# Seven edits at the stage boundaries of a fused two-block transformer kernel: first transfers, row sums, squares, and the order of the first slab

## The chip, the core and the metric

One NeuronCore of a Trainium2 chip runs the whole program. Its engines are TensorE (PE, with its weight loads as PEld), VectorE (DVE), ScalarE (ACT), GpSimd (POOL) and SyncE (SP); each runs its own instructions in order, and they wait for one another on semaphores. Weights come from HBM by DMA, which SP's and POOL's queues issue. The metric is the device time of one launch in microseconds (us), as the median of some runs; lower is better. Traces come from one further execution under the hardware profiler.

## The reference: what is computed

A token matrix of 256 x 1024 goes through two blocks of two layers each. Every sublayer has the form "norm over the 1024 features, matmul up, something in the middle, matmul down, add to x". All is float32.

```python
D_MODEL = 1024; SEQ = 256; DEPTH = 2; D_FF = 2816

def rms_norm(x, g):
    x32 = x.astype(jnp.float32)
    y = x32 * lax.rsqrt(jnp.mean(x32 * x32, axis=-1, keepdims=True) + EPS)
    return (y * g.astype(jnp.float32)).astype(x.dtype)

# first block, layer l: mixer (pool + attention, or RG-LRU), then the conv FFN
x = x + mixer(rms_norm(x, norm_mix[l]), ...)
z = causal_dwconv(rms_norm(x, norm_ffn[l]) @ w_in, conv_w, conv_b); u, g = jnp.split(z, 2, axis=-1)
x = x + (jax.nn.gelu(g) * u) @ w_out

# second block, layer i
cond = jax.nn.silu(c)
mod = (cond @ w_mod[i] + b_mod[i]).reshape(-1, N_SUBLAYERS, 3, D_MODEL)     # 1024 -> 9216
h = rms_norm_2(x, g) * (1.0 + scale[:, None, :]) + shift[:, None, :]        # modulate
x = x + 0.5 * gate * ((jax.nn.silu(h @ w_gate) * (h @ w_up)) @ w_down)      # FFN, before and after
x = x + gate * ssd_mixer(h)          # layer 0; mla_mixer(h) in layer 1
```

## The kernel before

**Layout.** x is kept transposed in SBUF as `X`, 128 partitions x 8 feature tiles x 256 tokens. The weights of all 22 matmul stages are cut into 271 slabs of 1 MB (128 x 2048). A slab has four times a place in the ring `raw` (4 buffers, filled by SP), then a high part `hi` made by ACT (`split_hi`, L814, two halves) and a low part `lo = raw - hi` made by DVE (`split_lo`, L1259, two halves), both in rings of 2. Each product is three matmuls: high weight x high input, high x low, low x high (`three`, L312 to L314); the four gated stages take high and low input side by side in one 512-wide matmul (`wide`, L347, L349). A slab is 48 such 256-wide products, or 16 wide and 16 narrow ones.

**Stages in order.** pa_in (8 slabs), pa_out (4), f0_up (22), f0_down (11), rg_in (10), rg_out (5), f1_up (22), f1_down (11), g00_up (22), g00_down (11), ssd_in (25), ssd_out (8), g01_up (22), g01_down (11), g10_up (22), g10_down (11), mla_in (3), mla_uq (4), mla_ukv (2), mla_out (4), g11_up (22), g11_down (11).

**A norm** stands ahead of ten of them (pa_in, f0_up, rg_in, f1_up, g00_up, ssd_in, g01_up, g10_up, mla_in, g11_up). ACT squares the eight tiles of X into `S` as the residual adds deliver them (L840, three pairs and two single tiles). DVE adds tiles 2,3 and then 4,5 to tiles 0,1 (`fold_squares`, L1278); in the code this stands ahead of the residual adds of the last two tiles (k = 3). PE sums over the features with one-column matmuls of tiles 0, 1, 6, 7 (L457; the trace has two records for each, 16 in all). ACT takes the root (L845), DVE the reciprocal and a diagonal matrix R, PE spreads it (L461). Then tile by tile DVE scales (L1346), ACT makes the high part (`xh_ready`, L851 or L853) and DVE the low part (`x_ready`, L1337 or L1339), and PE's first slab of the stage (`first_up_slab`, `gated_stage`) waits tile by tile for `x_ready`. pa_out and mla_out have no norm; there ACT and DVE make the two parts of the concatenated heads in pairs of tiles (L962 with `cat_hi`, L1501).

**A down stage** accumulates in PSUM banks 4 to 7; in its last slab PE finishes the outputs in pairs, and DVE adds each pair to X (`residual`, L1307, L1311, L1315). **The row sums** are `cond @ w_mod`: 144 units of 128 x 1024, each one a DVE instruction over a row of `modw` and `cond` (L1363), whose 512 KB come by SP through a ring of 3. They have no engine of their own and are spread over other stages by `MODS_PER`; `units_after` tells SP behind which slab the loads stand. In a down stage DVE does two after the split of every slab, the last of them after slab number SLABS-1, right ahead of the residual.

**The start.** SP issues X, the constants `CN`, the parameters `PAR`, four slabs and three row-sum units; POOL issues `cond`, positions and three tables. ACT, DVE and PE first wait until X, CN and PAR have all landed (`par_loaded`, 48).

## Time and profile before

| | us |
|---|---|
| median of 3 runs | 1985.22 (1983.73 to 1986.84) |
| the profiled execution, its whole time | 1992.79 |
| its span, first to last instruction | 1991.0 |
| PE busy | 1848.0 (93%) |
| DVE busy | 1440.8 (72%) |
| ACT busy | 1012.1 (51%) |
| TensorE clock granted, mean over the span | 0.943 of full |

PE is busy almost throughout; what is left is in short waits. The chain of waits, followed back from the last instruction, lies on PE for 85% of the span, on DVE for 8% and on ACT for 3%. A row of the timeline gives start, duration, engine, line, operation and, in brackets, how long the engine had been idle and what ended that. The granted clock is 1.00 (2.4 GHz) or 0.50 (1.2 GHz).

### The profile page before, as it was taken

The page shows a single profiled execution, that of the slowest core. Times are in us where ns is not written, and L with a number is a line of the kernel's source. Part 1 is how long each engine was busy: PE and PEld are TensorE (multiplying, and loading weights), DVE is VectorE, ACT ScalarE, POOL GpSimd, SP SyncE. Part 2 cuts the span into 40 slices and gives each one's busy share as a digit, 9 for nine tenths or more (in the row PEclk, how much of TensorE's full clock was granted, in tenths as well). Part 3 has the DMA queues.
Part 4 walks back from the last instruction along what each step waited for, and adds up shares of the span by engine and source line. Part 5 has one row for each costly group of instructions (what it writes and reads, how often), then busy time and mean ns, then how long its engine had stood idle before and what let it go on. Part 6 is the DMA issues. An engine that isn't in the chain of part 4 may idle for free.

```text
span 1991.0 us, 31981 instructions
## 1 busy us (share of the span) xinstructions
PE 1848.0 (93%) x12790; PEld 1697.5 (85%) x12790; DVE 1440.8 (72%) x2317; ACT 1012.1 (51%) x1582; POOL 18.5 (1%) x22
## 2 busy tenths in 40 slices
PE   6789999957999999999998999999999988899999
PEld 6579999857999888989996698889788987578899
DVE  4747888667788788889966758888888553656664
ACT  4445554563554455445557735553555344355542
POOL 2000000000000000000000000000000000000000
PEclk9799999888999999999998999999899977699999
DMA  8314459422455867884441035779577532014552
GB/s 311 116 43 167 172 193 348 156 106 85 170 187 213 317 228 263 307 321 170 174 166 42 1 127 190 268 287 364 200 276 287 209 107 105 22 43 169 184 180 101
DMA packets 61436, 367.15 MB, mean 184 GB/s; under 512 B 6832, under 2 KB 6832, under 8 KB 26384
## 3 DMA queue, kind: packets, MB, share of 16 engines
q1 hardware_dynamic: 60768, 362.67, 49.9%
q0 software_dynamic: 560, 3.01, 0.4%
q8 instruction: 71, 1.16, 0.2%
q14 instruction: 37, 0.30, 0.0%
HBM read 364.61 MB, written 1.05 MB: 184 GB/s over the span
## 4 chain that ended last, share of the span: by engine, by line
PE 85%; DVE 8%; ACT 3%; DMA 2%; issue 1%; SPq 0%; DVEq 0%; ACTq 0%
PE psum L347 17%; PE psum L312 16%; PE psum L313 16%; PE psum L314 16%; PE psum L349 9%; DVE lo L1259 2%; PE psum L660 1%; PE psum L470 1%; PE psum L611 1%; PE psum L494 1%; PE psum L711 1%; PE psum L457 1%; DMA modw<-wmod_dram 1%; ACT hi L814 1%; PE psum L482 1%
## 5 line engine op out<-in xcount | busy, mean ns | idle before, releaser
L1259 DVE TENSOR_TENSOR lo<-raw,hi 128x1024 fp32r<-128x1024 f32 x542 | 642.1, 1225 | 257.2 <-ACT hi L814 257.1
L814 ACT ACTIVATE hi<-raw 128x1024 fp32r<-128x1024 f32 x542 | 543.1, 1051 | 480.6 <-PE psum L314 475.8
L347 PE MATMUL psum<-XHL,hi 128*128 128x512 f32 x1408 | 505.9, 404 | 7.4 <-DVE XHL L1339 7.4
L312 PE MATMUL psum<-XHL,hi 128*128 128x256 f32 x1648 | 480.0, 291 | 20.5 <-DVE XHL L1337 7.1
L313 PE MATMUL psum<-XHL,hi 128*128 128x256 f32 x1648 | 474.2, 288 | 0.0
L314 PE MATMUL psum<-XHL,lo 128*128 128x256 f32 x1648 | 473.8, 287 | 0.0
L349 PE MATMUL psum<-XHL,lo 128*128 128x256 f32 x1408 | 399.0, 283 | 0.0
L312 PE MATMUL psum<-HH,hi 128*128 (+1 forms) x1264 | 361.4, 286 | 5.3 <-DVE lo L1259 5.3
L313 PE MATMUL psum<-HL,hi 128*128 (+1 forms) x1264 | 359.7, 285 | 0.0
L314 PE MATMUL psum<-HH,lo 128*128 (+1 forms) x1264 | 359.6, 284 | 0.0
L312 PEld LDWEIGHTS psum<-XHL,hi 128*128 128x128 f32 x1648 | 324.8, 197 | 26.7 <-issue 22.3
L347 PEld LDWEIGHTS psum<-XHL,hi 128*128 128x128 f32 x1408 | 268.7, 191 | 77.2 <-issue 9.8
L313 PEld LDWEIGHTS psum<-XHL,hi 128*128 128x128 f32 x1648 | 324.9, 197 | 1.3 <-issue 1.0
L314 PEld LDWEIGHTS psum<-XHL,lo 128*128 128x128 f32 x1648 | 324.4, 197 | 0.0
L349 PEld LDWEIGHTS psum<-XHL,lo 128*128 128x128 f32 x1408 | 270.1, 192 | 0.0
L312 PEld LDWEIGHTS psum<-HH,hi 128*128 128x128 f32 x1264 | 245.0, 194 | 5.9 <-issue 5.5
L313 PEld LDWEIGHTS psum<-HL,hi 128*128 128x128 f32 x1264 | 244.9, 194 | 0.1
L314 PEld LDWEIGHTS psum<-HH,lo 128*128 128x128 f32 x1264 | 244.7, 194 | 0.0
L1363 DVE CUSTOM_DVE_ANT_0 modw<-modw,cond 128x1024 f32<-128x1024 f32 x144 | 174.5, 1220 | 22.1 <-DMA modw<-wmod_dram 22.0
L907 ACT ACTIVATE S<-psum 128x512 f32<-128x512 f32 x88 | 52.6, 598 | 232.0 <-PE psum L349 232.0
L1434 DVE TENSOR_TENSOR S<-psum,S 128x512 f32<-128x512 f32 x88 | 60.9, 692 | 82.3 <-ACT S L907 82.0
L1403 DVE SCALAR_TENSOR_TENSOR S<-psum,PAR,S 128x254 f32<-128x254 f32 (+1 forms) x176 | 72.5, 474 | 0.0
(271 smaller groups left out, 1552.2 us busy)
## 6 DMA issues: line engine op xcount, KB each, us to landing
raw<-slabs_dram SPq DMA_DIRECT2D x271, 1024.0 KB, 4.8
modw<-wmod_dram SPq DMA_DIRECT2D x144, 512.0 KB, 5.8
A<-small_dram POOLq DMA_DIRECT2D x1, 1536.0 KB, 13.4
X<-x_dram SPq DMA_DIRECT2D x1, 1024.0 KB, 4.8
out_dram<-X SPq DMA_DIRECT2D x4, 256.0 KB, 2.3
cond<-cvec_dram POOLq DMA_DIRECT2D x1, 512.0 KB, 7.6
A<-tab_dram POOLq DMA_DIRECT2D x1, 512.0 KB, 16.7
PAR<-par_dram SPq DMA_DIRECT2D x1, 448.0 KB, 8.7
```

Of the source, the lines that this page charges most:

```text
L312: mm(dst, wh, xh, start=start, stop=False, skip_group_check=True)
L313: mm(dst, wh, xl, start=False, stop=False, skip_group_check=True)
L314: return mm(dst, wl, xh, start=False, stop=False, skip_group_check=True)
L347: mm(dst, hi[:, k, j * P:(j + 1) * P], XHL[:, kt, :, :].rearrange("p a t -> p (a t)"), start=start, stop=False, skip_group_check=True)
L349: return mm(dst[:, T:2 * T], lo[:, k, j * P:(j + 1) * P], XHL[:, kt, 0, :], start=False, stop=False, skip_group_check=True)
L457: last = mm(sums[:, j:j + 1], S[:, m * T + j * P:m * T + (j + 1) * P], ones[:, 0:1], start=(m == 0 and j == 0), stop=False, skip_group_che ...
L814: f(hi[:, n % SPLIT, at], raw[:, n % RAW, at], ACT.Copy).then_inc(q["hi_ready"], 1)
L907: f(S[:, 1024 + s % 2 * 512:1536 + s % 2 * 512].rearrange("p (a t) -> p a t", a=2), psum[:, b:b + 2, T:2 * T], ACT.Copy).then_inc(q["half_ ...
L1259: v.tensor_tensor(lo[:, n % SPLIT, at], raw[:, n % RAW, at], hi[:, n % SPLIT, at].bitcast(F32), ALU.subtract).then_inc(q["lo_ready"], 1)
L1363: v.tensor_tensor_reduce(out=w, in0=w, in1=cond[:, :], scale=1.0, scalar=0.0, op0=ALU.mult, op1=ALU.add, accum_out=MOD[:, n:n + 1]).then_i ...
L1403: last = stt(out=z, in0=bank[n % 4][:, m * T:(m + 1) * T - tap], scalar=col(f"fconv{layer}", (2 - tap) * 44 + k, i, 4), in1=z, op0=ALU.mul ...
L1434: v.tensor_tensor(two(dst), psum[:, b:b + 2, 0:T], two(S[:, 1024 + s % 2 * 512:1536 + s % 2 * 512]), ALU.add).then_inc(evacuated[s % 2], 1)
```

## The change

- **First transfers.** X comes in four parts of two tiles with a semaphore each, then the identity and ones columns of CN, slab 0 in two halves, PAR, slab 1, the rest of CN, slabs 2 and 3 and the row-sum units. POOL issues its five transfers after slab 1 has landed. ACT squares each pair as it lands; the copies to `identr`, `selr`, `maskr` (DVE) and the silu of `cond` (ACT) go behind slab 1 of pa_in.
- **Row sums.** A down stage does none behind its last split; ssd_out takes two after each of its first five splits, so that the 144 units still fit.
- **Squares.** DVE folds tiles 2,3 alone; PE sums tiles 0, 1, 4, 5, 6, 7: 12 one-column matmuls for 8.
- **First slab of a stage.** For tile kt PE takes the two products with the high input as soon as `xh_ready` (or `cat_hi`) allows, and the product with the low input of tile kt-1 behind it. In the gated stages the 512-wide matmul of the first slab becomes two of 256.

```diff
         "g10_up": "g10_down", "g11_up": "g11_down"}
-MODS_PER = {"f0_down": 2, "f1_down": 2, "g00_up": 2, "g00_down": 2, "g01_up": 2, "g01_down": 2,
+MODS_PER = {"f0_down": 2, "f1_down": 2, "g00_up": 2, "g00_down": 2, "ssd_out": 2, "g01_up": 2, "g01_down": 2,
             "g10_up": 2, "g10_down": 2}
...
         slabs, first = SLABS[name], N0[name]
-        last = [first + s + 2 for s in range(slabs - 2)] if name.endswith("down") else \
+        last = [first + s + 2 for s in range(slabs - 3)] if name.endswith(("down", "out")) else \
                [min(first + 2 * p + 3, NSLABS - 1) for p in range(slabs // 2)]
...
         @block.sync
         def _(sp):
-            sp.dma_start(X[:], x).then_inc(q["par_loaded"], 16)
-            sp.dma_start(CN[:], con).then_inc(q["par_loaded"], 16)
+            for k in range(4):
+                sp.dma_start(X[:, 2 * k:2 * k + 2, :], x[:, 2 * k:2 * k + 2, :]).then_inc(x_loaded[k], 16)
+            sp.dma_start(CN[:, 0:2 * P], con[:, 0:2 * P]).then_inc(q["ident_loaded"], 16)
+            sp.dma_start(raw[:, 0, 0:HALF], slabs[0][:, 0:HALF]).then_inc(q["slab_begun"], 16)
+            sp.dma_start(raw[:, 0, HALF:], slabs[0][:, HALF:]).then_inc(raw_loaded[0], 16)
             sp.dma_start(PAR[:], par).then_inc(q["par_loaded"], 16)
+            sp.dma_start(raw[:, 1, :], slabs[1]).then_inc(raw_loaded[1], 16)
+            sp.dma_start(CN[:, 2 * P:], con[:, 2 * P:]).then_inc(q["con_loaded"], 16)
             def load(k, n, i=None):
...
                 last.then_inc(q["slab_used"], 1)
+            def high_ready(preps, kt):
+
+                if preps in (2, 12):
+                    pe.wait_ge(q["cat_hi"], 4 * (preps // 12) + kt // 2 + 1)
+                else:
+                    pe.wait_ge(q["xh_ready"], KD * (norms[0] - 1) + kt + 1)
+
             def first_up_slab(stage, preps):
                 n = N0[stage]
                 pe.wait_ge(q["lo_ready"], 2 * n + 2)
-                for kt in range(KD):
-
-                    pe.wait_ge(q["x_ready"], KD * (preps - 1) + kt + 1)
-                    for m in range(2):
-                        last = three(bank[n % 4][:, m * T:(m + 1) * T], n, m * KD + kt,
-                                     XH[:, kt, :], XL[:, kt, :], start=(m == 0 and kt == 0))
+                b, k = bank[n % 4], n % SPLIT
+                for kt in range(KD + 1):
+                    if kt < KD:
+
+                        high_ready(preps, kt)
+                        for m in range(2):
+                            at = slice((m * KD + kt) * P, (m * KD + kt + 1) * P)
+                            for w in (hi, lo):
+                                mm(b[:, m * T:(m + 1) * T], w[:, k, at], XH[:, kt, :],
+                                   start=(m == 0 and kt == 0 and w is hi), stop=False, skip_group_check=True)
+                    if kt:
+
+                        pe.wait_ge(q["x_ready"], KD * (preps - 1) + kt)
+                        for m in range(2):
+                            at = slice((m * KD + kt - 1) * P, (m * KD + kt) * P)
+                            last = mm(b[:, m * T:(m + 1) * T], hi[:, k, at], XL[:, kt - 1, :],
+                                      start=False, stop=False, skip_group_check=True)
                 last.then_inc(q["slab_used"], 1)
             def wide(n, s, m, kt, start):
...
                 pe.wait_ge(q["lo_ready"], 2 * n + 2)
-                for kt in range(KD):
-                    pe.wait_ge(q["x_ready"], KD * (preps - 1) + kt + 1)
-                    for m in range(2):
-                        last = wide(n, 0, m, kt, kt == 0)
+                for kt in range(KD + 1):
+                    if kt < KD:
+
+                        high_ready(preps, kt)
+                        for m in range(2):
+                            at = slice((m * KD + kt) * P, (m * KD + kt + 1) * P)
+                            for w, half in ((hi, 0), (lo, T)):
+                                mm(psum[:, m, half:half + T], w[:, n % SPLIT, at], XH[:, kt, :],
+                                   start=(kt == 0 and half == 0), stop=False, skip_group_check=True)
+                    if kt:
+
+                        pe.wait_ge(q["x_ready"], KD * (preps - 1) + kt)
+                        for m in range(2):
+                            at = slice((m * KD + kt - 1) * P, (m * KD + kt) * P)
+                            last = mm(psum[:, m, T:2 * T], hi[:, n % SPLIT, at], XL[:, kt - 1, :],
+                                      start=False, stop=False, skip_group_check=True)
                 last.then_inc(q["slab_used"], 1)
                 for s in range(1, 4):
                     gated_slab(stage, s)
...
-                for m in (0, 1, 6, 7):
-                    if m >= 6:
+                for m in (0, 1, 4, 5, 6, 7):
+                    if m >= 4:
                         pe.wait_ge(q["squares_ready"], 8 * k + m + 1)
...
-            pe.wait_ge(q["par_loaded"], 48)
+            pe.wait_ge(q["ident_loaded"], 16)
             pe.wait_ge(q["zero_ready"], 1)
             norm()
...
                 if n >= NSLABS:
                     return
-                act.wait_ge(raw_loaded[n % RAW], plus(16 * (n // RAW + 1), i, 16))
+                if n == 0:
+                    act.wait_ge(q["slab_begun"], 16)
+                else:
+                    act.wait_ge(raw_loaded[n % RAW], plus(16 * (n // RAW + 1), i, 16))
                 if n >= SPLIT:
                     act.wait_ge(q["slab_used"], plus(n - SPLIT + 1, i, 4))
                 for h in range(2):
                     at = slice(h * HALF, (h + 1) * HALF)
+                    if n == 0 and h:
+                        act.wait_ge(raw_loaded[0], 16)
                     f(hi[:, n % SPLIT, at], raw[:, n % RAW, at], ACT.Copy).then_inc(q["hi_ready"], 1)
...
                         act.wait_ge(q["resid_ready"], 8 * (k - 1) + m + w)
+                    elif m < 7:
+                        act.wait_ge(x_loaded[m // 2], 16)
                     f(S[:, m * T:(m + w) * T], X[:, m:m + w, :].rearrange("p a t -> p (a t)"),
...
             act.wait_ge(q["zero_ready"], 1)
-            act.wait_ge(q["par_loaded"], 48)
-            norm("pa_in", then=ACT.Silu)
-            act.wait_ge(q["cond_loaded"], 16)
-            f(cond[:, :], cond[:, :], ACT.Silu).then_inc(q["cond_ready"], 1)
...
                     f(VRAW[:, 2 * (s - 6):2 * (s - 5), :],
                       bank[s % 4][:, :].rearrange("p (a t) -> p a t", a=2), ACT.Copy).then_inc(evacuated[s % 2], 1)
+                if s == 1:
+                    act.wait_ge(q["cond_loaded"], 16)
+                    f(cond[:, :], cond[:, :], ACT.Silu).then_inc(q["cond_ready"], 1)
                 if 3 <= s <= 6:
...
                     if s in between:
                         between[s]()
-                    modulation(mods)
+                    if s < SLABS[stage] - 3:
+                        modulation(mods)
             def fold_squares(k):
-                for pair in (1, 2):
-                    dve.wait_ge(q["squares_ready"], 8 * k + 2 * pair + 2)
-                    last = v.tensor_tensor(S[:, 0:2 * T], S[:, 0:2 * T], S[:, 2 * pair * T:2 * (pair + 1) * T],
-                                           ALU.add)
-                    if pair == 1:
-                        step.link(last)
-                last.then_inc(q["squares_folded"], 1)
+                dve.wait_ge(q["squares_ready"], 8 * k + 4)
+                v.tensor_tensor(S[:, 0:2 * T], S[:, 0:2 * T], S[:, 2 * T:4 * T],
+                                ALU.add).then_inc(q["squares_folded"], 1)
...
-            dve.wait_ge(q["par_loaded"], 48)
-            v.tensor_copy(identr[:, :], ident)
-            v.tensor_copy(selr[:, :], con_mat("select", 64))
-            v.tensor_copy(maskr[:, :], CN[:, CON["mask_f"]:CON["mask_f"] + 2 * P]).then_inc(q["identr_ready"], 1)
             fold_squares(0)
             split_lo(0)
+            dve.wait_ge(q["ident_loaded"], 16)
+            dve.wait_ge(q["par_loaded"], 16)
             norm("pa_in", "nmix0")
...
             for s in range(8):
                 split_lo(s + 2)
+                if s == 1:
+                    dve.wait_ge(q["con_loaded"], 16)
+                    v.tensor_copy(identr[:, :], ident)
+                    v.tensor_copy(selr[:, :], con_mat("select", 64))
+                    v.tensor_copy(maskr[:, :], CN[:, CON["mask_f"]:CON["mask_f"] + 2 * P]).then_inc(q["identr_ready"], 1)
                 if 3 <= s <= 6:
                     dve.wait_ge(q["qk_sum"], s - 2)
...
             group_rest(SSD_G - 1)
-            down_stage("ssd_out")
+            down_stage("ssd_out", mods=MODS_PER["ssd_out"])
             residual("ssd_out", 8)
...
             step.link(g.memset(UP[:, :, :, 0:PAD], 0.0))
+            pool.wait_ge(raw_loaded[1], 16)
             pool.dma_start(cond[:, :], cvec).then_inc(q["cond_loaded"], 16)
             pool.dma_start(posi[:, :], pos).then_inc(q["late_loaded"], 16)
```

What the change moves on three engines:

SP's queue at the program's start; X, CN, PAR, raw (the slabs) and modw (row-sum units) are the SBUF targets. Before:

```order
1 L274 DMA X<-x_dram 128x2048
2 L275 DMA CN<-con_dram 128x835
3 L276 DMA PAR<-par_dram 128x896
4 L285 DMA raw<-slabs_dram 128x2048 x4
5 L287 DMA modw<-wmod_dram 128x1024 x3
6 L282 DMA raw<-slabs_dram 128x2048 [waits lo_ready] x37
```

and now:

```order
1 L276 DMA X<-x_dram 128x512 x4
2 L277 DMA CN<-con_dram 128x256
3 L278 DMA raw<-slabs_dram 128x1024
4 L279 DMA raw<-slabs_dram 128x1024
5 L280 DMA PAR<-par_dram 128x896
6 L281 DMA raw<-slabs_dram 128x2048
7 L282 DMA CN<-con_dram 128x579
8 L291 DMA raw<-slabs_dram 128x2048 x2
9 L293 DMA modw<-wmod_dram 128x1024 x3
10 L288 DMA raw<-slabs_dram 128x2048 [waits lo_ready] x37
```

X stands in four parts, slabs 0 and 1 are ahead of or between PAR and the larger part of CN, and the transfers of row-sum units stay behind slab 3.

PE at the start of pa_in, from the last of the one-column matmuls over S, over the spread of R, into the first slab (psum<-XHL,hi and psum<-XHL,lo are high and low weights). Before:

```order
5 L457 MATMUL psum<-CN,S 128x1 [waits squares_ready]
6 L457 MATMUL psum<-CN,S 128x1
7 L461 MATMUL psum<-R,CN 128x256 [waits diag_ready]
8 L312 MATMUL psum<-XHL,hi 128x256 [waits x_ready,lo_ready]
9 L313 MATMUL psum<-XHL,hi 128x256
10 L314 MATMUL psum<-XHL,lo 128x256
11 L312 MATMUL psum<-XHL,hi 128x256
12 L313 MATMUL psum<-XHL,hi 128x256
13 L314 MATMUL psum<-XHL,lo 128x256
14 L312 MATMUL psum<-XHL,hi 128x256 [waits x_ready]
```

and now:

```order
9 L492 MATMUL psum<-CN,S 128x1 [waits squares_ready]
10 L492 MATMUL psum<-CN,S 128x1
11 L496 MATMUL psum<-R,CN 128x256 [waits diag_ready]
12 L357 MATMUL psum<-XHL,hi 128x256 [waits xh_ready,lo_ready]
13 L357 MATMUL psum<-XHL,lo 128x256
14 L357 MATMUL psum<-XHL,hi 128x256
15 L357 MATMUL psum<-XHL,lo 128x256
16 L357 MATMUL psum<-XHL,hi 128x256 [waits xh_ready]
17 L357 MATMUL psum<-XHL,lo 128x256
18 L357 MATMUL psum<-XHL,hi 128x256
19 L357 MATMUL psum<-XHL,lo 128x256
20 L364 MATMUL psum<-XHL,hi 128x256 [waits x_ready]
```

The first matmul of the slab waits for `xh_ready` in place of `x_ready`, and the first wait for `x_ready` comes after eight matmuls. The same order stands at every first slab. Where one listing of the norm had 8 rows of one-column matmuls it now has 12.

DVE at the end of f0_down, from the last row-sum units into the residual (X<-psum,X), the fold (S<-S) and the norm of rg_in. Before:

```order
265 L1259 TENSOR_TENSOR lo<-raw,hi 128x1024 x2
266 L1363 ISA modw,MOD<-modw,cond 128x1024
267 L1363 ISA MOD 128x1
268 L1363 ISA modw,MOD<-modw,cond 128x1024
269 L1363 ISA MOD 128x1
270 L1259 TENSOR_TENSOR lo<-raw,hi 128x1024
271 L1307 TENSOR_TENSOR X<-psum,X 128x512 x3
272 L1278 TENSOR_TENSOR S<-S 128x512 x2
273 L1311 TENSOR_TENSOR X<-psum,X 128x256 x2
274 L1259 TENSOR_TENSOR lo<-raw,hi 128x1024
```

and now:

```order
261 L1303 TENSOR_TENSOR lo<-raw,hi 128x1024 x2
262 L1404 ISA modw,MOD<-modw,cond 128x1024
263 L1404 ISA MOD 128x1
264 L1404 ISA modw,MOD<-modw,cond 128x1024
265 L1404 ISA MOD 128x1
266 L1303 TENSOR_TENSOR lo<-raw,hi 128x1024 x3
267 L1348 TENSOR_TENSOR X<-psum,X 128x512 x3
268 L1322 TENSOR_TENSOR S<-S 128x512
269 L1352 TENSOR_TENSOR X<-psum,X 128x256 x2
270 L1303 TENSOR_TENSOR lo<-raw,hi 128x1024
```

The two row-sum units behind the last full split are gone, and one of the two folds.

## Rows read from the trace of the kernel before

**Rows 1.** the page: the chain that ended last, by engine, share of the span

```profile
PE 85%; DVE 8%; ACT 3%; DMA 2%; issue 1%; SPq 0%; DVEq 0%; ACTq 0%
```

**Rows 2.** timeline from the start to pa_in's first matmul: start, us, engine, line

```profile
10.39 1.28 ACT L835 ACT_TABLE_LOAD   x1 [10.39 <-DMA PAR<-par_dram]
...
14.53 3.54 PE L457 MATMUL psum<-CN,S 128*128 128x1 f32 x16 [14.53 <-DVE S L1278]
...
15.92 2.00 ACT L814 ACTIVATE hi<-raw 128x1024 fp32r<-128x1024 f32 x2 [1.86 <-DMA raw<-slabs_dram]
...
18.11 0.26 ACT L845 ACTIVATE tiny<-psum,tiny 128x2 f32<-128x2 f32 x1 [0.18 <-PE psum L457]
...
19.74 2.00 ACT L814 ACTIVATE hi<-raw 128x1024 fp32r<-128x1024 f32 x2 [1.37 <-DMA raw<-slabs_dram]
...
20.02 1.22 PE L461 MATMUL psum<-R,CN 128*128 128x256 f32 x2 [1.95 <-DVE R L1329]
...
23.02 0.55 PE L312 MATMUL psum<-XHL,hi 128*128 128x256 f32 x1 [1.78 <-DVE XHL L1337]
```

**Rows 3.** transfers: KB each and us to landing; windows (us, PE busy, clock, DMA share, GB/s)

```profile
X<-x_dram SPq DMA_DIRECT2D x1, 1024.0 KB, 4.8
out_dram<-X SPq DMA_DIRECT2D x4, 256.0 KB, 2.3
...
10.00:14.00 4.00, 0.00 (x0) 1.00 1.02 431
...
26.00:30.00 4.00, 4.00 (x36) 1.00 1.03 420
```

**Rows 4.** timeline at the end of rg_out and the start of f1_up

```profile
489.66 0.75 DVE L1311 TENSOR_TENSOR X<-psum,X 128x256 f32<-128x256 f32 x2
...
489.80 1.95 PE L457 MATMUL psum<-CN,S 128*128 128x1 f32 x16 [0.94 <-DVE S L1278]
492.81 0.70 PE L461 MATMUL psum<-R,CN 128*128 128x256 f32 x2 [1.07 <-DVE R L1329]
...
494.07 1.20 ACT L851 ACTIVATE XHL<-S 128x256 fp32r<-128x256 f32 x3
...
495.30 0.55 PE L312 MATMUL psum<-XHL,hi 128*128 128x256 f32 x1 [1.78 <-DVE XHL L1337]
```

**Rows 5.** timeline at the end of f0_down and the start of rg_in

```profile
344.05 1.23 DVE L1363 CUSTOM_DVE_ANT_0 modw<-modw,cond 128x1024 f32<-128x1024 f32 x1 [2.24 <-DMA modw<-wmod_dram]
...
348.38 1.42 DVE L1278 TENSOR_TENSOR S<-S 128x512 f32<-128x512 f32 x2 [0.16 <-ACT S L840]
...
349.86 3.32 PE L457 MATMUL psum<-CN,S 128*128 128x1 f32 x16 [2.17 <-DVE S L1278]
...
357.25 0.55 PE L312 MATMUL psum<-XHL,hi 128*128 128x256 f32 x1 [1.78 <-DVE XHL L1337]
```

**Rows 6.** the one-column sums after f1_down, g00_down and pa_out

```profile
690.48 2.67 PE L457 MATMUL psum<-CN,S 128*128 128x1 f32 x16 [2.28 <-DVE S L1278]
...
889.58 1.95 PE L457 MATMUL psum<-CN,S 128*128 128x1 f32 x16 [1.82 <-DVE S L1278]
...
149.45 1.95 PE L457 MATMUL psum<-CN,S 128*128 128x1 f32 x16 [0.42 <-DVE S L1278]
```

**Rows 7.** windows around f0_down's end and f1_up's start (PE, PEld, DVE, ACT, POOL; clock; DMA)

```profile
347.70:350.15 2.45, 0.29 (x3) 0.30 (x3) 2.26 (x5) 1.25 (x3) 0.00 (x0) 1.00 0.66 269
350.16:353.20 3.04, 3.02 (x15) 2.93 (x14) 1.44 (x2) 0.75 (x2) 0.00 (x0) 0.50 0.12 16
...
495.30:500.30 5.00, 5.00 (x23) 5.00 (x24) 5.00 (x13) 3.46 (x7) 0.00 (x0) 0.50 0.10 36
```

**Rows 8.** timeline at pa_out's first slab

```profile
122.72 2.19 ACT L962 ACTIVATE XHL<-CAT 128x512 fp32r<-128x512 f32 x4
...
124.29 0.35 PE L312 MATMUL psum<-XHL,hi 128*128 128x256 f32 x1 [3.21 <-DVE XHL L1501]
```

**Rows 9.** timeline of DVE in ssd_out, one slab's split

```profile
1170.68 2.36 DVE L1259 TENSOR_TENSOR lo<-raw,hi 128x1024 fp32r<-128x1024 f32 x2 [3.40 <-ACT hi L814]
```

10 lines of the change are left out of this document (7 added, 3 removed).

## The prediction

> **What bounds the kernel now.** I read the page first, then the timeline of the places that the diff names, then the granted clock in windows. The chain by engine [rows 1] lies on PE for 85%: inside a stage PE is the bound, and nothing off PE is worth anything there. So I look only at where PE has nothing to do, and every edit aims at such a place. At the start, PE's first product of pa_in comes at 23.02 us, behind a string of waits: all engines wait for PAR until 10.39, the one-column sums end at 18.07, the high part of slab 1 (which ACT must make ahead of the first XH) waits for its transfer until 19.74 and ends at 21.74 [rows 2]. At a stage boundary the pattern is that of rg_out to f1_up [rows 4]: the last dense matmul ends at 488.86 (489.80 less 0.94 idle), the sums run 489.80 to 491.75, the spread of R starts at 492.81, the first product at 495.30. That is 6.44 us without a dense matmul. At f0_down's end it is 347.69 to 357.25, 9.56 us [rows 5]; there DVE was still at a row-sum unit at 344.05, after a wait of 2.24 us for its transfer, and came late to the residual and to the fold at 348.38.
>
> **First transfers.** What must be in before pa_in's first product is X, the identity part, slab 0, PAR and slab 1: 1024 + 128 + 1024 + 448 + 1024 = 3648 KB, 3.74 MB. X alone landed 4.8 us after its issue at about 0.74, so at 5.55 [rows 3]. The other 2.69 MB go at the 420 to 431 GB/s of the full queues [rows 3], 6.3 to 6.4 us, since POOL, whose transfers shared that rate before, now keeps still. I add 0.5 us for the smaller pieces: slab 1 is in at 12.4. ACT then makes its high part in 2.00 us [rows 2], to 14.5, and the first XH in 0.40 (a third of 1.20, [rows 4]); PE starts at 15.0. The other path gives nearly the same: squares done at 6.7, the fold by 5.7, 24 records of one-column sums at the cold rate of 3.54/16 = 0.22 each [rows 2], 5.3 us from 6.1 to 11.4, root 0.26, reciprocal and diagonal 0.8, spread 1.22, scaling 0.5: 14.3. I take 15.1, which is 7.9 us less than 23.02, the new order of the first slab included. Early end: 14.3, the other path alone (-8.7). Late end: slabs 0 and 1 take the 3.8 us each that lay between their arrivals before (15.92 and 19.74, [rows 2]) and not 2.5, so 17.7 (-5.3).
>
> What is moved is hidden. The three copies on DVE and the silu of cond on ACT, behind slab 1 of pa_in, stand where PE works 5.76 us on a slab (2.36 + 3.40, [rows 9]) and the splits take ACT 2.0 and DVE 2.36 of it. Uncovered they would cost 0.7 and 2.3 (a table load of 1.28 and half a split, 1.0, [rows 2]). POOL's transfers and the rest of SP's first ones, 6.9 MB together, follow 12.4 at 0.42 MB/us and are all in by 29 us; the tables' first user needs slabs 0 and 1 of pa_in worked off, 27 us at the earliest, and then has sums of its own to make. A few us of POOL's time would be lost, which nobody waits for.
>
> At one point the Trainium skill speaks against this. [Rows 3] show four 0.25 MB transfers landing 2.3 us after issue each and 1 MB after 4.8, and between 26 and 30 us, when half-size transfers of row-sum units are landing, 420 GB/s and a DMA share of 1.03: there is no hole between transfers that are queued together. The skill's page "DMA: Bandwidth & Descriptors" (section "Anatomy of one DMA") gives each transfer a fixed 2.0 us plus its bytes at 436 GB/s, and the section "Bandwidth" asks for 1 MB or more in each. Taken as a cost that adds up over the nine transfers it would be, as an estimate by that page, 18 us plus 8.6; the trace disagrees for queued transfers.
>
> **Row sums out of the last slab.** At f0_down, f1_down and g00_down, PE waited 2.17, 2.28 and 1.82 us for the fold where the stage without row sums shows 0.94 [rows 4 to 6]. With the units gone DVE follows each pair as in rg_out. ssd_out takes ten units: 2 x 1.23 us [rows 5] behind each of five splits, where DVE idles 3.40 us of every slab [rows 9]. Cost nothing; without the cover it would be up to 2.24 us (a late transfer, [rows 5]) a slab, of which about 1 us is in the slack.
>
> **Squares.** PE's eight further records cost 0.98 us warm (1.95/16 each, [rows 4]) and 1.77 cold (3.54/16, [rows 2]). But PE no longer waits for the second fold and starts as soon as its last dense matmul is out. At rg_out that gives 488.91 + 2.93 = 491.84 for 491.75: +0.1. ssd_out, g01_down and g10_down are alike, so +0.4 for four. At pa_out the wait is 0.42 only [rows 6]: 149.08 + 2.93 = 152.01 for 151.40, +0.6, and mla_out is the same: +1.2 for two. So this edit alone gains nothing; squares and residual come off the path and PE's own sums take their place. Together with the row sums: f0_down 347.69 to 350.67 warm, with the clock falling at 350.16 as before [rows 7] some 351.1, for 353.18: -2.1. f1_down 688.20 to 691.2 for 693.15: -2.0. g00_down 887.76 to 890.75 for 891.53: -0.8. The sum of the two edits is -4.9 + 1.6 = -3.3, and its ends are -6 (all warm, nothing added at the four) and +1 (each of the nine sums half cold).
>
> **High parts first.** PE's first product needs XH alone. In [rows 4] ACT delivers the first at 494.07 + 0.40, PE follows 0.07 later at 494.54 for 495.30: 0.76 earlier; the gated stages show the same to 0.05. The gain stays only if PE, not DVE, bounds the rest of the slab. The clock stood at 0.50 from 495.30 to 500.30 with PE busy for all 5.00 us and DVE too [rows 7]; a tile's six products then take 1.3 us, DVE's pair of operations 0.77, so PE is the bound and the start counts in full. (A product is 5.00/23 = 0.22, a DVE operation 5.00/13 = 0.38.) Warm, both need 0.72 (six of 5.76/48) and the end is set by the last low part: then the gain is four products, 0.48. Of the start that is won, a part is spent at half speed if the clock rises no sooner: 0.38 of 0.76. I take 0.74 for nine boundaries, -6.7 (ends -3.4 and -7). For pa_out and mla_out the first XH is there at 122.72 + 0.6, PE at 123.4 for 124.29 [rows 8]: -0.9 twice, -1.8. The 512-wide matmuls cut in two have the same columns; the 64 further weight loads lie under matmuls as all others do, +0.3 in all, between 0 and 1.
>
> **Sum.** -7.9 - 3.3 - 6.7 - 1.8 + 0.3 = -19.4. The profiled execution would go from 1992.8 (span 1991.0) to 1973.4. The runs shown lie 7.6 lower, 1985.2, with the same program; I take the difference over unchanged: 1965.8 us. The ends add to about -26 and -10; they will not all come together.
>
> **The rivals.**
> A. The start wins less: slab 1 is late, since the first nine transfers do not flow without holes. For: out's 0.25 MB take 2.3 us and 1 MB only 4.8 [rows 3]. If the nine ran one after the other, 4 x 2.3 + 2.3 + 3 x 3.5 + 4.8 = 26.8 us, PE would start 6 us later than now and the whole be 1965.8 + 7.9 + 6 = 1980; with holes for half of them, about 1971. Against: the full queues at 10 and 26 us. The page named above would give the 1980 too.
> B. The clock takes back the early starts. The time of a first slab is set by how long the clock stays at 0.50 [rows 7]. If every rise keeps its old place, the nine boundaries and the two without a norm keep half of what the high parts gain: 1965.8 + 3.4 + 0.9 = 1970. For: the level is granted in stretches that do not follow the kernel. Against: a rise can come sooner as well as later, and over eleven boundaries that should come out even.
> C. DVE becomes the bound in ssd_out: 2.36 + 2.46 + 2.24 = 7.1 us for a slab of 5.76, five times 1.3 = 6.5: 1972. Against: a late transfer in every slab would be needed; without one it is 4.8 us.
> D. Slower. The 24 sums start right behind the last dense matmul; if the clock falls there and not 2.4 us later as in [rows 7], sums and spread run cold: 5.3 for 2.93 and 1.22 for 0.70 [rows 2, 4], 2.9 us at nine boundaries, 26: 1992. It decides from about 2.6 us a boundary. Against: in [rows 7] the clock was still 1.00 through 2.45 us in which PE did almost nothing.
> E. The edits don't do what they say: PE's first product still comes with the low part, because ACT makes slab 1's high part ahead of XH and is late. Against: in [rows 4] ACT had that part ready and XH began at 494.07, 0.56 after the spread was out (493.51), which is about the time of one scaling. If it does not fit, the 6.7 are lost: 1972.5.
>
> **How the numbers follow.** My forecast 1965.8 has 0.72 (its own range 1961 to 1970), A 0.08, B 0.08, C 0.03, D 0.03, E 0.04, and 0.02 for what I do not see. What a measurement of this kernel can tell from no change is about 0.2%, 4 us. All but D, the worst of A and a mixture of mishaps end below 1981: faster 0.94, same 0.03, slower 0.03. The range 1960 to 1972.5 holds the forecast, B, most of A and C.
>
> **What would show it.** Right: PE's first product of pa_in near 15 us, with ACT's high part of slab 1 waiting for its transfer until about 12.4; PE's idle time before the one-column sums below 0.2 us at all nine boundaries, with 24 records in 2.9 us; 5.7 us from the last dense matmul to the first product, at f0_down and f1_down at most 6.5; the first product released by ACT's XH; no wait of PE inside ssd_out. Wrong: a start after 18 us; a clock of 0.50 within 2 us of the last dense matmul; PE idle in ssd_out; a first slab that ends no earlier, counted from the last dense matmul.

## The result and the profile after

The changed kernel took 1975.7 us (median of 11 runs, 1973.0 to 1981.9), the kernel before beside it 1983.9 (11 runs, 1977.4 to 1989.4): ratio 0.9961 [0.9945, 0.9977]. It is faster, but by 8 us and not by 19; 1975.7 lies outside the range 1960 to 1972.5.

The profiled executions differ by what was forecast: 1973.84 us for the changed kernel, 1992.79 before, 19.0 less. That agreement is an accident. Over the whole study the kernel before ran 90 times beside others: mean 1984.8, standard deviation 4.2, from 1973.5 to 1994.6. The execution shown ahead of the prediction was one of its slowest, and that of the changed kernel was the third fastest of its eleven. Nearly 11 of the 19 us lie between the two profiled executions and the means of their kernels (1992.8 against 1984.8; 1973.8 against 1976.5).

The page of the changed kernel: the span, PE's busy time, the granted clock by fortieths of the span, and the chain by engine [rows 1]:

```profile
span 1971.9 us, 32258 instructions
...
PE 1855.0 (94%) x12934; PEld 1708.9 (87%) x12934; DVE 1438.0 (73%) x2307; ACT 1011.8 (51%) x1581; POOL 18.5 (1%) x22
...
PEclk9799999978999899999998999999899987799999
...
PE 87%; DVE 7%; ACT 3%; DMA 1%; issue 1%; SPq 0%; DVEq 0%; ACTq 0%
```

PE's share of the chain rose from 85 to 87%: less of the path lies off PE, as intended. The timeline of the start answers to [rows 2] (start, us, engine, line; in brackets the idle time before and what ended it):

```profile
7.21 5.29 PE L492 MATMUL psum<-CN,S 128*128 128x1 f32 x24 [7.21 <-DMA CN<-con_dram]
...
14.15 2.00 ACT L856 ACTIVATE hi<-raw 128x1024 fp32r<-128x1024 f32 x2 [1.36 <-DMA raw<-slabs_dram]
...
16.07 1.01 ACT L895 ACTIVATE XHL<-S 128x256 fp32r<-128x256 f32 x3
...
16.61 0.55 PE L357 MATMUL psum<-XHL,hi 128*128 128x256 f32 x1 [1.72 <-ACT XHL L895]
```

pa_in begins at 16.61 in place of 23.02: 6.4 us won, 1.5 less than the forecast's 7.9 (15.1). The chain is the one that was forecast, but slab 1 is in at 14.15 and not at 12.4. The windows of DMA say why (us; PE, PEld, DVE, ACT, POOL busy; clock; DMA share; GB/s): where the prediction took 420 GB/s, the queue moved 290 and 243.

```profile
2.00:5.00 3.00, 0.00 (x0) 0.00 (x0) 0.00 (x0) 1.11 (x4) 0.00 (x0) 1.00 0.97 290
5.00:8.00 3.00, 0.79 (x4) 0.79 (x4) 0.69 (x1) 1.72 (x4) 0.00 (x0) 1.00 0.92 243
8.00:11.00 3.00, 3.00 (x16) 3.00 (x15) 0.66 (x1) 1.52 (x2) 0.00 (x0) 1.00 1.04 424
```

At the boundaries, the timeline of PE behind rg_out and f1_down, which answers to [rows 4, 6]:

```profile
478.92 2.84 PE L492 MATMUL psum<-CN,S 128*128 128x1 f32 x24
482.83 1.22 PE L496 MATMUL psum<-R,CN 128*128 128x256 f32 x2 [1.07 <-DVE R L1370]
485.17 0.55 PE L357 MATMUL psum<-XHL,hi 128*128 128x256 f32 x1 [1.11 <-ACT XHL L895]
...
677.38 3.09 PE L492 MATMUL psum<-CN,S 128*128 128x1 f32 x24
681.55 1.22 PE L496 MATMUL psum<-R,CN 128*128 128x256 f32 x2 [1.07 <-DVE R L1370]
683.98 0.55 PE L401 MATMUL psum<-XHL,hi 128*128 128x256 f32 x1 [1.21 <-ACT XHL L897]
```

No idle time is left ahead of the sums (0.94 and 2.28 before), and the wait between spread and first product fell from 1.78 to 1.11 (f1_up) and from 1.84 to 1.21 (g00_up), released by ACT's high part. But the spread took 1.22 and not 0.70 us: the clock had already fallen. From the last dense product to the first product of the next stage, summed over the nine boundaries with a norm, the trace has 67.6 us before and 57.2 after: 10.4 less, where the prediction's terms make 10.0 (3.3 and 6.7). The first slabs behind them, counted from the first product of a slab to the first product of the next, take 69.4 us before and 69.3 after. So within these two executions the boundaries came out as forecast, and the start 1.5 us short of it. The timed runs say otherwise, and the experiments had to find what the two executions hide.

### The profile page after: what moved, and what is told of

Same layout as the page of the kernel before. It is cut to its first block, busy times and chain, and to the rows that moved or that the text cites. A ratio compares the mean times of both kernels' runs of the same rounds, so it can differ in the third digit from the quotient of the medians.

```text
span 1971.9 us, 32258 instructions
## 1 busy us (share of the span) xinstructions
PE 1855.0 (94%) x12934; PEld 1708.9 (87%) x12934; DVE 1438.0 (73%) x2307; ACT 1011.8 (51%) x1581; POOL 18.5 (1%) x22
## 3 DMA queue, kind: packets, MB, share of 16 engines
HBM read 364.61 MB, written 1.05 MB: 185 GB/s over the span
## 4 chain that ended last, share of the span: by engine, by line
PE 87%; DVE 7%; ACT 3%; DMA 1%; issue 1%; SPq 0%; DVEq 0%; ACTq 0%
PE psum L372 16%; PE psum L319 16%; PE psum L320 16%; PE psum L321 16%; PE psum L374 8%; PE psum L357 2%; PE psum L697 1%; DVE lo L1303 1%; PE psum L492 1%; PE psum L505 1%; PE psum L401 1%; PE psum L648 1%; PE psum L529 1%; PE psum L748 1%; PE psum L364 1%; ACT hi L856 1%
## 5 line engine op out<-in xcount | busy, mean ns | idle before, releaser
L372 PE MATMUL psum<-XHL,hi 128*128 128x512 f32 x1344 | 475.1, 399 | 0.0
L319 PE MATMUL psum<-XHL,hi 128*128 128x256 f32 x1520 | 438.1, 288 | 4.5 <-ACT A L1264 3.9
L320 PE MATMUL psum<-XHL,hi 128*128 128x256 f32 x1520 | 433.5, 285 | 0.0
L321 PE MATMUL psum<-XHL,lo 128*128 128x256 f32 x1520 | 433.4, 285 | 0.0
L374 PE MATMUL psum<-XHL,lo 128*128 128x256 f32 x1344 | 378.1, 281 | 0.0
L372 PEld LDWEIGHTS psum<-XHL,hi 128*128 128x128 f32 x1344 | 252.8, 188 | 62.8
L319 PEld LDWEIGHTS psum<-XHL,hi 128*128 128x128 f32 x1520 | 292.7, 193 | 6.1 <-DVE lo L1303 4.1
L320 PEld LDWEIGHTS psum<-XHL,hi 128*128 128x128 f32 x1520 | 292.7, 193 | 1.3 <-issue 1.0
L321 PEld LDWEIGHTS psum<-XHL,lo 128*128 128x128 f32 x1520 | 292.6, 193 | 0.0
L374 PEld LDWEIGHTS psum<-XHL,lo 128*128 128x128 f32 x1344 | 254.4, 189 | 0.0
```

Of the source, the lines that this page charges most:

```text
L319: mm(dst, wh, xh, start=start, stop=False, skip_group_check=True)
L320: mm(dst, wh, xl, start=False, stop=False, skip_group_check=True)
L321: return mm(dst, wl, xh, start=False, stop=False, skip_group_check=True)
L372: mm(dst, hi[:, k, j * P:(j + 1) * P], XHL[:, kt, :, :].rearrange("p a t -> p (a t)"), start=start, stop=False, skip_group_check=True)
L374: return mm(dst[:, T:2 * T], lo[:, k, j * P:(j + 1) * P], XHL[:, kt, 0, :], start=False, stop=False, skip_group_check=True)
```

## The experiments

Means are given with their standard error, since the differences are small. Kernels of one group ran on one chip; the mean of the kernel before was 1983.9 to 1987.0 in these groups. Where a difference is taken between kernels of two groups, its ± does not hold what the chips may differ by, up to 3 us by these means.

### One part at a time

c_before is the kernel before once more, timed as a kernel of its own. e_start has the first transfers alone, e_high the high parts first alone, e_rows the row sums out of the last slab alone:

```
-            sp.dma_start(X[:], x).then_inc(q["par_loaded"], 16)
+            for k in range(4):
+                sp.dma_start(X[:, 2 * k:2 * k + 2, :], x[:, 2 * k:2 * k + 2, :]).then_inc(x_loaded[k], 16)
 ...                                                          (e_start)
-                    pe.wait_ge(q["x_ready"], KD * (preps - 1) + kt + 1)
+                        high_ready(preps, kt)
 ...                                                          (e_high)
-                    modulation(mods)
+                    if s < SLABS[stage] - 3:
+                        modulation(mods)
 ...                                                          (e_rows)
```

> The kernel before, unchanged, as a control. Theory 1 (the traced execution of before was a slow draw: TensorE's clock stood at 0.50 in unlucky places): a second trace of the same program shows the same waits of PE at start and at the nine stage boundaries to 0.1 us wherever the clock is the same, but other stretches at 0.50, and a span of 1977 to 1986 instead of 1991.0; the span follows the time that dense matmuls spend at 0.50. Rival (the trace is typical and the edits are worth less in ordinary runs): span again 1988 or more in the trace, while timed runs lie near 1984.

> Before with the new first transfers alone. Both theories: PE's first product of pa_in at 17.3 us (16.61 in the changed kernel plus 0.7 for the low part) for 23.02, so 5.7 us less in the trace. Theory 1: 5 to 6.5 us less in the timed median. Rival (the start's gain is given back, e.g. at the tail of pa_in whose chain waits for something else): under 3 us.

> Before with the high parts first in every first slab, nothing else. Theory 1: PE's wait ahead of the first product falls by 0.67 to 0.74 at ten norms and by 0.8 at two stages without one, and the timed median by 8 us. Rival (the clock rises no sooner, so a part of the earlier start is spent at half speed, or the slab's end is set by its last low part): 3 to 5 us.

> Before with the row sums taken out of the last slab of each down stage and ten units put into ssd_out. Theory 1: PE's wait ahead of the one-column sums goes from 2.2 to 1.0 us after f0_down and f1_down and from 1.8 to 1.05 after g00_down, and the sums no longer run cold there; 3 to 5 us less in the timed median. Rival: under 2 us, because in ordinary runs those sums were not cold, or because ssd_out pays (PE idle inside it).

| kernel | mean us (12 runs) | ratio to before |
|---|---|---|
| c_before | 1986.8 ± 1.1 | 1.0015 [1.0000, 1.0030] |
| e_start | 1980.6 ± 0.8 | 0.9974 [0.9957, 0.9992] |
| e_high | 1986.2 ± 0.8 | 1.0012 [0.9998, 1.0026] |
| e_rows | 1984.6 ± 0.9 | 1.0002 [0.9989, 1.0014] |

The control shows what such a comparison can tell: 0.15% here for a program that is the same. Against the control the start is worth 6.2 us, the row sums 2.2, the high parts 0.6, each ± 2.8 (95%). The control itself was 2.7 us slower than the 35 runs of the same program beside it. Against all 47 runs of the unchanged program on this chip (mean 1984.8) the start is worth 4.3 ± 2.1, the row sums 0.2 ± 2.3, and the high parts cost 1.4 ± 2.1. So only the start is told from nothing. The high parts, counted at 8.2, are the term that is missing by either measure; their rival of 3 to 5 us missed too. For the row sums the rival (under 2 us) fits as well as any gain, although the waits that they aimed at are gone in the trace of e_rows (0.94, 0.94 and 1.05 us behind f0_down, f1_down and g00_down).

The theory on c_before, that the traced execution of before was slow by its clock, did not hold: c_before's trace has a span of 1986.5 us, 4.5 less, with 230.8 us at half clock where before had 226.3. In the timed runs the two do go together: over 78 of the 79 runs of before for which the clock is on record (one was left out, whose clock of 0.90 does not fit its time) each microsecond at half clock goes with 0.57 us of time, with a correlation of 0.85.

The traces of e_high look well all the same: the wait between spread and first product is 0.63 to 0.68 us shorter at every boundary (1.11 or 1.21 for 1.78 or 1.85). What becomes of it is seen at g01_up, which starts 5.98 us behind the last dense product in e_high and 6.61 before. Timeline and windows of e_high, whose last dense product ended at 1191.74:

```profile
1195.81 0.70 PE L490 MATMUL psum<-R,CN 128*128 128x256 f32 x2 [1.07 <-DVE R L1358]
1197.72 0.55 PE L395 MATMUL psum<-XHL,hi 128*128 128x256 f32 x1 [1.21 <-ACT XHL L882]
...
1197.72:1203.69 5.97, 5.97 (x28) 5.97 (x29) 5.97 (x15) 4.56 (x9) 0.00 (x0) 0.50 0.20 81
```

and the same windows of the kernel before, whose last dense product ended at 1198.28:

```profile
1198.28:1203.49 5.21, 2.65 (x19) 2.16 (x18) 3.74 (x9) 3.17 (x6) 0.00 (x0) 1.00 0.17 50
...
1204.90:1210.31 5.41, 5.41 (x17) 4.64 (x18) 5.41 (x13) 4.00 (x8) 0.00 (x0) 0.50 0.07 29
```

The clock comes back 12.04 us behind the last dense product before and 11.95 in e_high. The slab that began 0.63 us earlier spent 5.97 us at 0.50 in place of 5.43, and the slab behind it began 0.34 us earlier, 14.43 us behind the last dense product in place of 14.77. That is rival B, seen at a boundary where the clock fell at the same place in both. Over the nine boundaries a first slab had 4.99 us at half clock in e_high, 4.68 in c_before and 4.33 in the trace of before. This accounts for some 1.5 to 3 us in these traces and not for all of the 8.2. The rest of the loss is in no trace: from the last dense product to the second slab the nine boundaries take 130.7 us in e_high, 136.2 in c_before and 137.0 before, so e_high's own trace shows 5.6 us or more of gain, in an execution (1981.8) that was 4.5 us faster than the mean of its kernel. Nor do the runs show more time at half clock: 222 ± 2 us in e_high, 224 ± 2 in c_before, 217 ± 1 in the 35 runs of before. So the clock itself had to be tried.

### Holding the clock up, first attempt: fillers that wait too long

Fillers are dense matmuls into a bank that nobody reads, at the nine boundaries, in TensorE's waits; the output is as before:

```
+            def keep(stage, at, count):
+                n = N0[stage]
+                pe.wait_ge(q["lo_ready"], 2 * n + 2)
+                for _ in range(count):
+                    mm(bank[at][:, 0:T], hi[:, n % SPLIT, 0:P], hi[:, n % SPLIT, 0:T], start=True, stop=True, ...)
```

> The kernel before, plus filler matmuls (256 columns, the next slab's own high part as weights and as moving tile, into a PSUM bank that nobody reads) at the nine boundaries between stages: 6 before the sums (2 after pa_out and mla_out), 8 between sums and spread, 13 between the spread and the first product, in places where TensorE waited in the trace of before. No part of the change is in it. Theory 1 (the granted clock falls at each boundary because TensorE has little to do there, and some 4.3 to 4.7 us of each first slab then run at half speed): with the clock at 1.00 through the boundary a first slab loses 2 us less, but the halves of the norm that come from VectorE (0.73 us for one of eight tiles) pace it, so 1 to 2 us at each of nine boundaries, 10 to 18 us faster than before; the first slabs show no clock of 0.50, and the runs of this kernel spread less than those of before (sd 4.5 us). Theory 2 (the clock falls whatever fills the gaps, as the sums of one column, 2 us, are there still): the time is that of before within 2 us, or up to 2 us slower by fillers that run longer than the wait they fill.

> The same fillers (6, 8, and 8 in place of 13 where the wait is now shorter) with the high parts first in each first slab, no other part of the change. Alone and without fillers the high parts first gave 1.0012 [0.9998, 1.0026], though the trace shows each first product 0.6 to 0.7 us earlier after its spread. Theory 1 (the first products start earlier, into a stretch at half clock, and the clock comes back at an hour that the start does not move, so the gain is taken back): with the clock held, the earlier start counts: 5 to 6 us below the kernel with fillers and the low parts in the old order. Rival (the order is worth nothing because VectorE paces the slab: the last low part comes at the same time as before and the slab ends behind it): the two kernels with fillers are equal within 1.5 us, and the first slab with high parts first ends at the same distance from the last dense product. Theory 2 of the run before: no gain from either.

> The changed kernel with its squares as before, and the fillers at the nine boundaries (6 or 2 before the sums, 8 behind them, 8 behind the spread). If theory 1 holds, the clock at the boundaries and the earlier starts count together: 10 to 18 us below the same kernel without fillers, 1957 to 1965. If the clock falls all the same (theory 2), the time is that of the same kernel without fillers within 2 us.

Measured, in the order of these three: 2011.0 ± 1.7 (ratio 1.0133 [1.0114, 1.0152]), 2011.0 ± 2.7 (1.0149) and 2001.0 ± 1.3 (1.0088). Both theories missed. The granted clock was 0.50 for 6.8 or 10.2 us at all nine boundaries of e_warm_before. Its timeline behind rg_out:

```profile
497.41 0.28 PE L314 MATMUL psum<-HH,lo 128*128 128x256 f32 x1
500.43 1.65 PE L453 MATMUL psum<-hi 128*128 128x256 f32 x6 [2.73 <-DVE lo L1273]
501.87 3.41 PE L469 MATMUL psum<-CN,S 128*128 128x1 f32 x16
505.14 2.05 PE L453 MATMUL psum<-hi 128*128 128x256 f32 x8
```

The fillers wait for the second half of the next slab's low part, which DVE makes behind the residual. TensorE stood still for 2.73 us, the clock fell 1.9 us behind the last dense product, and the sums (3.41 for 1.95) and the fillers ran at half speed on the path. The attempt says nothing on theory 1; it shows that a filler with a wait of its own is a new wait.

### Second attempt

Fillers wait for the first half (`2 * n + 1`), and they are fewer. e_after_fold2, of the group of the first attempt, is the changed kernel with its squares undone and no filler; the suffix after2 is that kernel.

```
+                keep(stage, spare, 6 if bank_of_sums == 3 else 2)
                 pe.wait_ge(q["squares_folded"], k + 1)
 ...             (the sums)
+                keep(stage, spare, 7)
                 pe.wait_ge(q["diag_ready"], k + 1)
                 mm(bank[4][:, 0:T], ones, R[:, 0:T], start=True, stop=True).then_inc(q["spread_ready"], 1)
+                keep(stage, spare, 12)            (7 where high parts go first)
```

> The kernel before with fillers at the nine boundaries, as the run e_warm_before, but the fillers wait only for the first half of the next slab's low part (the second is made behind the residual, and waiting for it held TensorE still for 3.0 us), and they are 6 (2 after pa_out and mla_out) before the sums, 7 behind them and 12 behind the spread, so that at 0.12 us each (0.21 at half clock) they fit into the waits of 1.05, 1.06 and 1.78 us. Theory 1 (the clock falls for want of work on TensorE): the clock falls at none or few of the boundaries; where it stays, the first slab takes 5.9 us in place of 8, and the kernel is 5 to 15 us faster than before. Theory 2 (it falls all the same because the sums of one column, 2 to 3 us, stay): cold time in a first slab as before (4.3 to 4.7 us), the time within 2 us of before, or up to 4 us slower where fillers at half clock overrun their waits.

> The same fillers (6, 7 and 7) with the high parts first, no other part of the change. Theory 1: 5 to 6 us below the kernel with fillers and the old order, as each first product comes 0.6 to 0.7 us earlier and the clock has nothing to take back. Rival (the order alone is worth nothing, since the last low part of the norm comes no earlier): within 1.5 us of it. Theory 2 (fillers do not hold the clock): within 2 us of it.

> The changed kernel with its squares as before, and the fillers 6 (or 2), 7 and 7. Without fillers this kernel took 1972.2 us. Theory 1: 1958 to 1967. Theory 2: 1970 to 1975.

> As e_fill_after2, and one filler more behind each of the sums but the last two, so that TensorE has no stretch of one-column products alone at a boundary. It adds six fillers of 0.12 us to the path of the sums, 0.7 us at a boundary and 6.5 us in all. Theory 1 in its strict form (dense work right through keeps the clock at 1.00): no clock of 0.50 at all nine boundaries, first slabs of 5.9 us, so 9 times 2.1 to 2.8 us less cold time against 6.5 us: 1953 to 1962. If the clock falls here too, what it follows is not TensorE's work: 1976 to 1984.

| kernel | mean us | ratio to before | profiled: first slabs, us at half clock, sum of nine |
|---|---|---|---|
| e_fill_before | 1970.4 ± 1.7 | 0.9928 [0.9906, 0.9949] | 1.6 (before: 39.0) |
| e_fill_high | 1964.3 ± 1.7 | 0.9905 [0.9880, 0.9930] | 5.2 (e_high: 44.9) |
| e_fill_after2 | 1958.4 ± 1.1 | 0.9875 [0.9851, 0.9899] | 4.5 (e_after_fold2: 47.5) |
| e_dense_after2 | 1965.9 ± 1.3 | 0.9914 [0.9892, 0.9937] | 0.5 |

Theory 1 holds for the time and only in part for the clock. The kernel before gains 14 us by matmuls whose results nobody uses, which theory 2 does not allow. But the clock still fell at seven of nine boundaries in e_fill_before and at five in e_fill_high, where "none or few" was expected; it fell for 3.4 us (once 6.8) in place of 6.8 or 10.2, so that little of it was left for the first slabs. The boundary into g01_up in e_fill_high, last dense product at 1182.16:

```profile
1182.00 0.88 PE L482 MATMUL psum<-hi 128*128 128x256 f32 x6
1183.21 1.95 PE L498 MATMUL psum<-CN,S 128*128 128x1 f32 x16 [0.34 <-DVE S L1321]
1185.02 1.08 PE L482 MATMUL psum<-hi 128*128 128x256 f32 x7
1186.23 0.70 PE L503 MATMUL psum<-R,CN 128*128 128x256 f32 x2
1186.57 1.18 PE L482 MATMUL psum<-hi 128*128 128x256 f32 x7
1188.13 0.36 PE L395 MATMUL psum<-XHL,hi 128*128 128x256 f32 x1 [0.38 <-ACT XHL L896]
...
1194.54 0.50 PE L366 MATMUL psum<-XHL,hi 128*128 128x512 f32 x1 [0.43 <-DVE lo L1302]
...
1188.13:1194.65 6.52, 6.09 (x49) 5.89 (x50) 6.52 (x16) 5.11 (x11) 0.00 (x0) 1.00 0.17 70
```

The first product comes at the same distance, 5.97, as in e_high, the clock stays at 1.00, and the second slab (L366) follows 6.41 us later where it took 8.45. DVE, busy for all of the window, now sets the slab's length, as the prediction said of a warm slab: PE waits 0.43 us for DVE's low part of the next slab.

e_fill_high is 6.1 ± 2.4 us (standard error) below e_fill_before; no gain at all is out by 2.6 standard errors, the rival's bound of 1.5 us by 2.0. This difference is not the order of the products alone. The two kernels also differ in their fillers behind the spread, 12 and 7: the 12 kept PE from the first product, its input being ready, for 1.9 us over the nine boundaries of the trace, the 7 for 0.6. At the two boundaries where the clock stayed at 1.00 in both traces, the second slab begins 11.78 us behind the last dense product in place of 12.26 (f1_up) and 12.38 in place of 12.64 (g01_up). That is 0.48 and 0.26 us of gain from starts that came 0.67 and 0.64 earlier: 0.2 and 0.4 us are lost even with the clock held (PE waits for DVE ahead of the second slab for 0.04 and 0.43). Nine such boundaries would make 2.3 to 4.3 us, as an estimate from these two.

The clock did not stay up in the others either: in e_fill_after2 it fell at six of nine boundaries, for 3.4 us each, of which 0.1 to 2.0 us reached into four of the first slabs. e_dense_after2 holds it at seven of nine, and the six fillers among the sums cost what they put on the path: 7.5 ± 3.4 us (95%) more, where 6.5 was worked out. Its time lies between the two forecasts, 1953 to 1962 and 1976 to 1984. In e_fill_after2 the half-clock time in first slabs was 4.5 us in all, so there was little left to buy back at that price.

### The squares, and the other terms with the clock held

> The changed kernel with its squares as before: VectorE folds the squares twice, and TensorE sums 8 columns pairs in place of 12. The prediction put the squares alone at +1.6 us: eight more half microseconds of sums on the path against a fold that is no longer waited for. By its rows the changed kernel without them is 1 to 3 us faster than the changed kernel, near 1973. Rival (in the changed kernel the sums start directly behind the last dense product and TensorE has more work there, so that the clock stays up in more of the first slabs: 0.50 for 4.25 us of a first slab there against 4.33 to 4.99 where the squares are the old ones): 1 to 4 us slower than the changed kernel, 1977 to 1980.

> The changed kernel whole, its new sums of squares too, with fillers behind the sums (7) and behind the spread (7); none ahead of the sums, which start directly behind the last dense product there. It is e_fill_after2 with the squares of the change in place of the old ones. The prediction has the squares at +1.6 us; without fillers the kernels with and without them stood at means of 1976.5 and 1972.6 us. If what they cost is the path (24 sums records in place of 16 from 1.0 us earlier: the sums end 0.0 to 0.2 us later, 2.9 to 3.1 us behind the last dense product against 2.4 to 3.0): +1 to +2 us against e_fill_after2, 1959 to 1961. If it is the clock (3 us of one-column products behind dense work, longer than 2): the clock falls at more boundaries than in e_fill_after2, where it fell at six of nine, and the time is 4 to 8 us above it, 1962 to 1967.

> e_fill_high with the new first transfers: high parts first, start, old row sums, old squares, fillers. Against e_fill_high (mean 1964.3) it prices the start with the clock held. By the traces the first product comes 5.7 us earlier (17.31 and 17.27 against 23.02 and 22.53 to 23.14), and the dense work behind it is the same: -5.3 to -5.8 us, 1958.5 to 1959. By the term of the prediction it would be -7.9, 1956.4.

> e_fill_high with the row sums out of the last slab and one row-sum stage at ssd_out. Against e_fill_high it prices the row sums with the clock held; alone without fillers they gave 1.0002 [0.9989, 1.0014]. By the waits before the sums in e_fill_high (0.94, 0.93, 0.94, 1.64 us behind f0_down, f1_down and at g00 and ssd_in, where 0.94 and 1.05 are what the fold alone makes) only one boundary of that trace had a stall left, of 0.6 us: so -0.6 us, and up to -3 where a draw has the late modulation weights at three boundaries, as e_fill_before had. If they are free of any effect: within 1 us.

e_after_fold2 took 1972.6 ± 1.0 (0.9944 [0.9928, 0.9960]), 3.9 less than the changed kernel; e_fill_after 1963.0 ± 1.0 (0.9887), 3.8 more than e_fill_after2 (1959.2 ± 0.6 with its repetition below). So the new squares cost 3.9 ± 2.7 us (95%) without fillers and 3.8 ± 2.3 with them, where 1.6 was forecast. (The second pair also differs in the 6 or 2 fillers ahead of the sums, which e_fill_after does not have. Its clock fell at seven of nine boundaries, and its time lies above the forecast for the path alone, 1959 to 1961.) With fillers the trace shows 2.0 of it on the path: the nine distances from the last dense product to the first product sum to 56.8 us against 54.8, above all at f1_up, where the clock fell inside the sums:

```profile
477.83 2.50 PE L504 MATMUL psum<-CN,S 128*128 128x1 f32 x17
480.19 1.84 PE L488 MATMUL psum<-hi 128*128 128x256 f32 x7
481.83 1.05 PE L509 MATMUL psum<-R,CN 128*128 128x256 f32 x2
482.33 2.06 PE L488 MATMUL psum<-hi 128*128 128x256 f32 x7
484.18 0.41 PE L357 MATMUL psum<-XHL,hi 128*128 128x256 f32 x1
```

Without fillers the traces do not show where the 3.9 us are (the profiled executions stand at 1973.8 and 1973.2).

e_fill_high_start took 1962.5 ± 1.2 (0.9882) and e_fill_high_rows 1963.1 ± 1.0 (0.9882). Against e_fill_high the start gives 1.8 ± 2.1 and the rows 1.2 ± 2.0; against e_fill_after2, which has both, leaving the start out costs 3.9 ± 1.2 and leaving the rows out 3.3 ± 1.3. All of these pairs are of two groups. The start was expected at 5.3 to 5.8 here; neither price excludes that. The terms, forecast and measured (us, ± 95%; in brackets against all 47 runs of the unchanged program):

| term | forecast | alone, against the control | with fillers |
|---|---|---|---|
| start | -7.9 | -6.2 ± 2.7 (-4.3 ± 2.1) | -1.8 ± 4.2; -3.9 ± 2.4 |
| row sums | -4.9 | -2.2 ± 2.8 (-0.2 ± 2.3) | -1.2 ± 4.0; -3.3 ± 2.6 |
| squares | +1.6 | +3.9 ± 2.7 (in the changed kernel) | +3.8 ± 2.3 |
| high parts first | -8.2 | -0.6 ± 2.7 (+1.4 ± 2.1) | -6.1 ± 4.7 (fewer fillers too) |
| further weight loads | +0.3 | not timed alone | |
| sum | -19.4 | -5.1 (+0.8); the whole change -7.7 | |

The -4.9 and the +1.6 are split by boundary and not by edit: -4.9 stands for both edits at the three boundaries with row sums, +1.6 for the squares at the other six. Only their sum of -3.3 can be held against a measurement, and it is +1.7 or +3.7 by the middle column.

### Why slab 1 was late

c_fill_after2 is e_fill_after2 again, on the chip of the other two, in which only X's first transfers differ:

```
-            for k in range(4):
-                sp.dma_start(X[:, 2 * k:2 * k + 2, :], x[:, 2 * k:2 * k + 2, :]).then_inc(x_loaded[k], 16)
+            sp.dma_start(X[:], x).then_inc(x_loaded[0], 16)        (e_x_one; e_x_two: two of 4 * k:4 * k + 4)
```

> The kernel of e_fill_after2 once more (the changed kernel with the old squares and fillers; X in four transfers of 2 KB a partition), as the measure for the two that differ in the transfers of X alone. Theory: 1958 +/- 3 us; DMA moves 240 to 290 GB/s from 2 to 8 us and 420 behind that; the first product of pa_in at 16.6 to 17.3.

> The same with X in two transfers (4 KB a partition). Theory P (small pieces slow the queue: 290 and 243 GB/s from 2 to 8 us in the changed kernel, where before had 408 with X whole): the rate from 2 to 8 us rises to 330 to 400, slab 1 is in 0.5 to 1 us sooner than the 14.15 us of the changed kernel, the first product of pa_in comes 0.5 to 1 us sooner, and the time falls as much. Rival (the first microseconds are slow whatever is sent, or other pieces are to blame): the rates and the first product as in the control, within 0.3 us.

> The same with X in one transfer (8 KB a partition), as in the kernel before, but alone ahead of the rest. Theory P: 400 GB/s from 2 to 8 us, slab 1 in at 12.5 to 13.3, its high part at 14.5 to 15.3, the first product at 15.0 to 15.8, as the prediction had it (15.1), 1.5 us faster than the control. The squares begin 1 us later, but do not bind. Rival: no change at slab 1, and by the later squares the first product comes 0 to 1 us later.

| kernel | mean us | GB/s 2 to 5, 5 to 8 us | slab 1's high part begins | first product |
|---|---|---|---|---|
| c_fill_after2 | 1959.8 ± 0.3 | 281, 241 | 14.41 | 16.87 |
| e_x_two | 1957.3 ± 0.3 | 313, 332 | 14.11 | 16.57 |
| e_x_one | 1956.5 ± 1.4 | 337, 323 | 13.23 | 15.69 |

The windows and the timeline of e_x_one:

```profile
2.00:5.00 3.00, 0.00 (x0) 0.00 (x0) 0.00 (x0) 0.22 (x2) 0.00 (x0) 1.00 0.86 337
5.00:8.00 3.00, 0.00 (x0) 0.00 (x0) 1.13 (x2) 2.28 (x5) 0.00 (x0) 1.00 0.97 323
...
13.23 2.00 ACT L869 ACTIVATE hi<-raw 128x1024 fp32r<-128x1024 f32 x2 [0.99 <-DMA raw<-slabs_dram]
...
15.69 0.55 PE L356 MATMUL psum<-XHL,hi 128*128 128x256 f32 x1 [1.35 <-ACT XHL L908]
```

Theory P holds for X in one piece: the first product comes 1.2 us earlier than in c_fill_after2, of the 1.8 by which that kernel missed the forecast's 15.1, and inside the 15.0 to 15.8 that were expected, though the rate stayed below the 400 GB/s. X in two pieces came 0.3 us earlier where 0.5 to 1 was expected, which is the rival's bound, and 16.57 is no earlier than the 16.61 of the changed kernel with four; e_fill_after2, the same program as c_fill_after2, had 17.27. These are single executions. In e_x_one the rate still stays at 323 between 5 and 8 us, so something else takes a part (perhaps slab 0 in halves, or the constants); that was not tried. In the runs e_x_two is 2.5 ± 0.9 us (95%) below c_fill_after2 and e_x_one 3.3 ± 2.8, which is more than the start shows, and where it comes from is open. The Trainium skill's page "DMA: Bandwidth & Descriptors" (section "Bandwidth") advises transfers of 1 MB or more. The prediction set it aside by rows in which large transfers were queued. Its figures, and the fixed price of 2.0 us in the section that the prediction names, are for transfers that GpSimd issues, and these are SP's. The runs of e_x_one agree with the page in direction for the first microseconds, and not with its fixed price per transfer added up: in the changed kernel slab 1 was in at 14.15 us and not at the 26 or so that the sum would give.

e_x_two at 1957.3 and e_x_one at 1956.5 have the lowest means of the study, some 30 us or 1.5% below the kernel before beside them (0.9848 [0.9820, 0.9877] and 0.9849 [0.9821, 0.9876]), and 19 to 20 below the changed kernel, which ran in another group.

## Why the prediction was wrong

- **Direction and the pattern of waits: right.** PE idles less than 0.2 us ahead of the sums at all nine boundaries. The sums of 24 records take 2.84 at rg_out's end where 2.93 was worked out. The first product is released by ACT, and ssd_out with its row sums shows one wait of PE, of 0.3 us.
- **"PE is the bound and the start counts in full": the step that failed.** The prediction counted 0.74 us at nine boundaries, and 8.2 us in all with pa_out and mla_out. The earlier starts came (0.63 to 0.68 us at the nine, 0.80 at pa_out), but they did not count in full. The prediction saw that the clock could spend the win and gave that rival 8% and a price of 4.3 us, on the ground that a rise can come sooner as well as later. Timed alone the edit gave 0.6 ± 2.7 us against the control. What the traces show in place of the step: at g01_up, with the clock falling at the same place, 0.34 of 0.63 us was left; with the clock at 1.00 throughout, 0.26 to 0.48 of 0.64 to 0.67, since DVE then sets the slab's end. With fillers the edit gave 6.1 ± 4.7. That points to the clock, but the two results differ by 5.5 ± 5.3 us only, across chips, and the second holds fewer fillers too. So the traces show, boundary by boundary, that a good part of each earlier start is lost, to the clock or to DVE. Why the runs without fillers show next to nothing of the 8.2 is open.
- **Squares +1.6: mis-sized, +3.9.** The working priced the records warm, with TensorE busy at once behind the dense work. In the changed kernel the spread at rg_out's end already stood at half clock (1.22 for 0.70). But over the nine boundaries it was wholly or partly at half clock eight times there and seven times before, so this is a small part of the 2.3 us at most; the rest is open.
- **Row sums -4.9 (the two edits together -3.3): mis-sized, somewhere from nothing to -3.** The stalls of 2.17 and 2.28 us behind f0_down and f1_down [rows 5, 6] were those of one execution: c_before had 1.51 and 1.72 in the same places, e_high 1.40 and 0.94. At g00_down it was the other way (1.82 before, 2.21 and 2.35). They depend on when a transfer lands, and the forecast took one execution's as a constant.
- **Start -7.9: mis-sized, -5.7 to -6.4 in the traces and 2 to 6 in the runs.** Slab 1 came at 14.15 and not at 12.4, since the queue moved 290 and 243 GB/s from 2 to 8 us and not 420. Sending X whole brought back 1.2 us of it; what else slowed the queue is open.
- **The forecast of the profiled execution was met by luck.** It was 1973.4, and the profiled execution took 1973.84. The base of 1985.2 was sound (mean of 90 runs 1984.8). But the waits were read from an execution 8 us slower than the mean, and the one of the changed kernel was 2.7 us faster than its mean. How much this pulled the terms is shown for the row sums alone; the waits behind the start and the high parts were the same in c_before (23.14 us; 1.78 to 1.85). The range of 1960 to 1972.5 allowed for one term failing and not for several that fell short together.

## What to carry to other kernels

- Where a slab behind a gap runs at half clock, first ask what brings the clock back, and which engine sets the end of the slab once it is back. An earlier start may only lengthen the slow stretch. Dense matmuls without effect, put where TensorE waits anyway, gave this kernel more (14 us) than the whole change (8 us).
- Such fillers must not wait for anything that comes later than the work behind them, and must fit their gap at the lower clock too.
- Read a stall in more than one execution before its removal is priced, and time the unchanged kernel beside the experiments, more than once.

## What the runs showed of the hardware

- The program without any change spreads over 21 us (1973.5 to 1994.6 in 90 runs), 1% of its time, and most of it goes with the time at half clock (correlation 0.85). With fillers the spread of e_fill_after2's repetition was 2.0 us (six runs, 1958.5 to 1960.5), though e_x_one, otherwise alike, had 8.5 and e_fill_before 10.4.
- A TensorE that works on one-column products without a gap did not keep its clock. Behind f1_down in the changed kernel PE was busy for all of the 2.42 us from the first sum on, and the clock fell at 679.83, inside the sums, which ended at 680.48:

```profile
677.38:679.80 2.42, 2.42 (x22) 2.42 (x22) 1.89 (x3) 0.82 (x3) 0.00 (x0) 1.00 0.02 7
679.83:690.00 10.17, 7.89 (x34) 7.11 (x34) 7.84 (x20) 7.42 (x13) 0.00 (x0) 0.50 0.29 103
```

- Stretches at half clock last 6.8 or 10.2 us at the boundaries of the unfilled kernels and 3.4 or 6.8 at those of the second attempt. How far they reach into a first slab differs from boundary to boundary: 2.8 to 6.2 us without fillers.
- With X in four transfers the queue moved 241 to 300 GB/s between 2 and 8 us, with X in two 313 and 332, with X in one 337 and 323, with a DMA share of 0.84 or more in all: the engines are busy either way, and the share does not tell how much they move.
